# The end of a decoder step on one core: the last attention phase, the samples' row copies and the final layer norms in another order

## The reference

```
def forgetting_attention_mixer(h, k, v, c_k, c_q, q_pos, k_pos, w_in, b_in, w_out, b_out):
    p = h @ w_in + b_in
    q = p[..., :FA_WIDTH].reshape(n, s, FA_HEADS, FA_HEAD_DIM)
    z = p[..., FA_WIDTH:]
    o = ...                      # softmax(q k / 8 + decay) v, block by block
    return (o * jax.nn.silu(z)) @ w_out + b_out
...
x = layer_norm(DEEPNORM_ALPHA * x + (1.0 + gate) * f, ln_g[layer], ln_b[layer])
```

## Time and profile before

| | us |
|---|---|
| median of 3 runs (lowest to highest) | 1718.39 (1717.39 to 1720.2) |
| the profiled execution | 1719.35 |
| its span | 1717.9 |
| PE busy in the span | 1635.8 |
| DVE, ACT, POOL busy | 1008.8, 635.7, 425.1 |

### The profile page before, as it was taken

How to read it: one execution, slowest core, us unless ns; L and a number is a source line. 1 busy time by engine, 2 the same in 40 slices (tenths; PEclk the granted TensorE clock), 3 DMA queues, 4 the chain that set the end, 5 groups by cost and what they waited for, 6 DMA issues and landing times.

```text
span 1717.9 us, 27999 instructions
## 1 busy us (share of the span) xinstructions
PE 1635.8 (95%) x10128; PEld 1425.0 (83%) x10128; DVE 1008.8 (59%) x1564; ACT 635.7 (37%) x1002; POOL 425.1 (25%) x421
## 2 busy tenths in 40 slices
PE   5999999999999998999989999999999999988996
PEld 3899999999999998899977777777778787866764
DVE  3432343334333436424566889788888878688836
ACT  2221221121112115324444545463646363645224
POOL 0250011101101110000221525262626262423130
PEclk9999999999999998999999999999999999999998
DMA  9491112122222220323523242424241422251694
GB/s 371 140 332 49 42 63 87 67 95 76 73 85 74 85 87 24 114 101 108 168 88 118 97 122 88 110 86 112 72 123 61 123 74 86 61 161 44 235 374 170
DMA packets 88674, 199.48 MB, mean 116 GB/s; under 512 B 17106, under 2 KB 47954, under 8 KB 86818
## 3 DMA queue, kind: packets, MB, share of 16 engines
q1 hardware_dynamic: 74898, 139.35, 25.1%
q0 software_dynamic: 13712, 59.30, 9.5%
HBM read 172.88 MB, written 34.39 MB: 121 GB/s over the span
## 4 chain that ended last, share of the span: by engine, by line
PE 77%; DVE 11%; issue 4%; ACT 4%; POOL 2%; DMA 2%; SPq 0%; DVEq 0%; ACTq 0%; POOLq 0%
PE bank L1973 20%; PE bank L1975 19%; PE bank L1974 19%; PE bank L2342 2%; PE bank L2108 2%; PE bank L2344 2%; PE bank L2343 2%; PE bank L2296 2%; DVE bank L1609 2%; PE bank L2324 2%; PE bank L2323 2%; POOL p_lo L726 1%; PE bank L2088 1%; PE bank L2199 1%; DMA xT<-x_t 1%
## 5 line engine op out<-in xcount | busy, mean ns | idle before, releaser
L1973 PE MATMUL bank<-h_hi,w_lo 128*128 128x344 f32 x1152 | 373.8, 324 | 8.6 <-DVE h_lo L1248 8.6
L1974 PE MATMUL bank<-h_lo,w_hi 128*128 128x344 f32 x1152 | 367.9, 319 | 0.0
L1975 PE MATMUL bank<-h_hi,w_hi 128*128 128x344 f32 x1152 | 367.6, 319 | 0.0
L726 POOL TENSOR_TENSOR p_lo<-parg,p_hi 128x512 fp32r<-128x512 f32 (+1 forms) x192 | 229.0, 1210 | 157.5 <-ACT p_hi L1083 157.2
L1973 PEld LDWEIGHTS bank<-h_hi,w_lo 128*128 128x128 f32 x1152 | 216.9, 188 | 13.9 <-issue 9.3
L1973 PE MATMUL bank<-x_hi,w_lo 128*128 128x512 f32 x528 | 219.9, 416 | 0.9 <-DVE x_lo L1683 0.8
L1974 PEld LDWEIGHTS bank<-h_lo,w_hi 128*128 128x128 f32 x1152 | 216.9, 188 | 0.2 <-issue 0.2
L1975 PEld LDWEIGHTS bank<-h_hi,w_hi 128*128 128x128 f32 x1152 | 216.6, 188 | 0.0
L1975 PE MATMUL bank<-x_hi,w_hi 128*128 128x512 f32 x528 | 208.2, 394 | 0.0
L1974 PE MATMUL bank<-x_lo,w_hi 128*128 128x512 f32 x528 | 208.1, 394 | 0.0
L1205 DVE TENSOR_TENSOR w_lo<-raw,w_hi 128x1024 fp32r<-128x1024 f32 x108 | 146.5, 1356 | 80.8 <-ACT w_hi L813 79.7
(11 more groups left out here) (320 smaller groups left out, 2636.5 us busy)
## 6 DMA issues: line engine op xcount, KB each, us to landing
raw<-units SPq DMA_DIRECT2D x124, 512.0 KB, 3.6
scr_k<-cache_k POOLq DMA_DIRECT2D x32, 512.0 KB, 5.7
ada_ring<-w_ada SPq DMA_DIRECT2D x32, 512.0 KB, 3.3
kpb<-scr_k SPq DMA_DIRECT2D x24, 512.0 KB, 4.1
pages<-cache_v POOLq DMA_DIRECT2D x20, 512.0 KB, 6.1
ada_first<-w_ada SPq DMA_DIRECT2D x8, 1024.0 KB, 15.2
ckb<-scr_c POOLq DMA_DIRECT2D x16, 512.0 KB, 4.6
KX<-KA SPq DMA_DIRECT2D x32, 256.0 KB, 6.6
```

The lines of the kernel that those rows point to most:

```text
L726: g.tensor_tensor(p_lo[:, r, off:HALF], parg[:, r, off:HALF], p_hi[:, r, off:HALF].bitcast(F32), ALU.subtract).then_inc(S("p_ready"), 1)
L1973: mm(out, lhs_lo, rhs_hi, start=first, stop=False)
L1974: mm(out, lhs_hi, rhs_lo, start=False, stop=False)
L1975: return mm(out, lhs_hi, rhs_hi, start=False, stop=last)
```

## The change

Four things are written in another order; what is computed is the same.

1. End of the last phase. ACT splits y's part 2 before the last probabilities, and parts 3 to 6 right after them, ahead of the weight unit `hi(U_FA + 1)`; DVE's `lo(U_FA + 1)` goes behind them. Part 7 is split by halves of the tokens: the first before the weight unit (it was divided long before), the second after the last division. `gates(1, ...)` moves ahead of the first half.
2. PE takes part 7 of pieces 0 and 1 apart, with k = 4..6 of piece 2 in between, so that piece 2 has only k = 7 left later.
3. The samples' `tok` copies go from DVE to ACT; the transposes of v and f follow piece 4 and not piece 3.
4. The tail. ACT takes the sums of tiles 3, 4 and 6 (before: 3, 5 and 7), DVE those of 5 and 7. The gate-and-copy of pieces 16 and 17 (`fg2`) comes ahead of the x-hats of tiles 3 and 4, the transposes of tile 7 ahead of the samples' projection, and `sample_rows_act` behind the x-hat of tile 7.

```diff
-        ACT_TILES = (3, 5, 7)
+        ACT_TILES = (3, 4, 6)
         TILE_PAIR = (1, 1, 1, 1, 2, 1, 0, 2)
+        TILE_AFTER = (0, 1, 2, 3, 0, 4, 0, 5)
...
+            def last_y2_high(half):
+                cs = slice(half * HALF, half * HALF + HALF)
+                act.wait_ge(S("o_step"), 8 * KB - 4 + 4 * half)
+                A(y2_hi[:, KB - 3, cs], y2T[:, KB - 1, cs], ACT.Copy).then_inc(S("y2_hi"), 1)
...
                     kq_high(j + 1, 0)
+                else:
+                    y2_high(2)
                 probs(j, 11)
...
                 else:
+                    for k in range(3, KB - 1):
+                        y2_high(k)
+                    last_y2_high(0)
                     hi(U_FA + 1, (U_FA + 1) % 2, (U_FA + 1) // 2 + 1, "mm", 12 * KB)
-                    for k in range(2, KB - 1):
-                        y2_high(k)
                 take_sums(j, 1)
...
-            y2_high(KB - 1)
+            last_y2_high(1)
+            def tok(n, dst, src):
+                act.wait_ge(S("tok_mm"), n)
+                A(dst[:, :], pair(src)[0:NS, :], ACT.Copy).then_inc(S("tok_ready"), 1)
...
+                if m == 2:
+                    tok(1, qtok, 2)
+                    tok(2, ktok, 3)
+                if m == 4:
+                    tok(3, vtok, 2)
...
-                if m in TILE_AT:
-                    if TILE_AT[m] in ACT_TILES:
-                        tile_sums(TILE_AT[m])
+                if m in (11, 12, 13):
                     layer_norm_act(TILE_AT[m], TT, xh2(TILE_AT[m]), "yo_ready")
-            layer_norm_act(6, TT, xh2(6), "yo_ready")
+                if m == 15:
+                    tile_sums(3)
+                if m == 16:
+                    layer_norm_act(3, TT, xh2(3), "yo_ready")
+                    tile_sums(4)
+            for t in (4, 5):
+                layer_norm_act(t, TT, xh2(t), "yo_ready")
+            tile_sums(6)
+            for t in (6, 7):
+                layer_norm_act(t, TT, xh2(t), "yo_ready")
             sample_rows_act()
-            tile_sums(7)
-            layer_norm_act(7, TT, xh2(7), "yo_ready")
...
                 else:
-                    lo(U_FA + 1, (U_FA + 1) % 2)
                     for k in range(2, KB - 1):
                         y2_low(k)
+                    gates(1, "fa_b_out")
+                    last_y2_low(0)
+                    lo(U_FA + 1, (U_FA + 1) % 2)
...
-            gates(1, "fa_b_out")
-            y2_low(KB - 1)
+            last_y2_low(1)
...
                     finish(3)
-                    gated_s()
-                    layer_norm_stats(4, TT)
+                    tile_scale(4)
+            gated_s()
+            layer_norm_stats(5, TT)
             finish(4)
-            tile_scale(5)
-            layer_norm_stats(6, TT)
             finish(5)
+            tile_scale(6)
+            layer_norm_stats(7, TT)
+            finish(6)
             dve.wait_ge(S("fs_used"), 3)
...
-            finish(6)
-            tile_scale(7)
             norm_sum(rS[:, :, :], KB)
             finish(7)
...
-                    fa_first(KB - 1)
+                    pe.wait_ge(S("y2_split"), KB)
+                    fa_step(0, KB - 1).then_inc(S("fa_mm"), 1)
+                    for k in range(KB // 2, KB - 1):
+                        fa_step(2, k)
+                    pe.wait_ge(S("y2_split"), KB + 1)
+                    fa_step(1, KB - 1).then_inc(S("fa_mm"), 1)
...
-                if m == 3:
+                if m == 4:
                     pe.wait_ge(S("tok_ready"), 2)
                     turn(2, 2)
...
             ln_forward(6, r2T, TT)
+            ln_forward(7, r2T, TT)
             pe.wait_ge(S("d_step"), 5)
...
-            ln_forward(7, r2T, TT)
```

More of the change, by code:

```diff
@@ L1545, in y2_low, with last_y2_low @@
                     .then_inc(S("y2_split"), 1)
-            def tok(n, dst, src):
-                dve.wait_ge(S("tok_mm"), n)
-                v.tensor_copy(dst[:, :], pair(src)[0:NS, :]).then_inc(S("tok_ready"), 1)
+            def last_y2_low(half):
+                cs = slice(half * HALF, half * HALF + HALF)
+                dve.wait_ge(S("y2_hi"), KB + half)
+                v.tensor_tensor(y2_lo[:, KB - 1, cs], y2T[:, KB - 1, cs], y2_hi[:, KB - 3, cs].bitcast(F32), ALU.subtract)\
+                    .then_inc(S("y2_split"), 1)
             def by_key(q, c):
@@ L1917, in _ @@
                 if m == 2:
-                    tok(1, qtok, 2)
-                    tok(2, ktok, 3)
                     score_late(4)
                 if m == 3:
-                    tok(3, vtok, 2)
                     score_late(5)
@@ L2131, in ln_forward @@
                 elif n0:
-                    wait(pe, S("ln_hat"), n0 + t if 0 < t < TT // 2 else n0 + t - 1)
+                    wait(pe, S("ln_hat"), n0 + TILE_AFTER[t])
                 else:
@@ L2373, in fa_first @@
                 for half in range(2):
-                    last = fa_step(half, k)
-                    if k == KB - 1:
-                        last.then_inc(S("fa_mm"), 1)
+                    fa_step(half, k)
             def phase(j, more):
@@ L2505, in _ @@
                     pe.wait_ge(S("fg2_ready"), m - 1)
-                    for k in range(KB // 2 if m in (2, 3) else 0, KB):
+                    for k in range({2: KB - 1, 3: KB // 2}.get(m, 0), KB):
                         last = fa_step(m, k)
```

## The result

| | before | changed |
|---|---|---|
| median of 4 runs each (lowest to highest) | 1719.3 (1717.39 to 1721.25) | 1710.32 (1709.78 to 1713.23) |
| the profiled execution | 1719.35 | 1713.23 |
| its span | 1717.9 | 1711.7 |

The measured ratio is 0.9943, with a 95% interval of 0.9929 to 0.9957: faster. The two medians differ by 9.0 us, where 6.1 was forecast; their own quotient is 0.9948. The two profiled executions differ by 6.12 us; the forecast was built on the first of them.

A forecast was written before the change was run, and what follows sets the result against it. PE, busy 1635.8 of 1717.9 us, was taken to bound the kernel, except where unfed or where ACT and DVE set the end. Up to the scores 5.3 plus 0.8 behind gave 6.1 us: 1718.39 to 1712.3, range 1710.0 to 1714.9.

The forecast's parts named there:

- Splits, copies, the head's sum: Up to the scores' transposes: PE waits of 2.2, 0.3 and 2.8 us go, minus 5.3 us, bounds 4.3 and 5.6.
- DVE just follows: DVE's queue up to the gathered scores becomes 5.45 us earlier, enough for PE's 5.3 us to count.
- The division stays at its time: End of the last phase: part 7's first half and the gates fill idle time, moving the last division within 0.1 us.
- Margins: Before the scores: weight unit's low part ready 0.9 us before PE wants it, copy of v 0.8 us before DVE arrives.
- The contention at part 2: y's part 2 on DVE beside POOL's last p_lo costs 0.5 us more, still ahead of PE; sum unchanged.
- Tail: Scores' transposes to the end: minus 2.3 us at full speed, 1.5 given back by a slow samples' fold, minus 0.8.
- Rival A: PE's clock stays up towards the program's end, which gains 2.3 us: 7.6 us in all, 1710.8; chance 0.19.
- B: DVE's extra statistics eat the end's gain and an earlier margin is missed: 3.8 to 5.3 us less, 1713.9; chance 0.24.
- C: Slower: new_key on DVE waits for ACT's copy of v; 8 us late gives 1719.5; chance 0.03.
- D: PE's waits return at the weight unit and scores, the end costs 1 us: some 2 us less, 1716.4; chance 0.04.
- The median of the runs lies 0.96 under the profiled one: Whole kernel: median before taken as 1718.39 us against 1719.35 profiled, so the changed median becomes 1712.3.
- half a microsecond for the median's own spread: Whole kernel: allowance of half a microsecond in the forecast's range, 1710.0 to 1714.9 us.

The follow-up runs named there:

- The copies-only kernel: Kernel before with only the samples' copies moved to ACT and the transposes of v and f behind piece 4; 1716.88 us, ratio 0.9986.
- its repeat: The kernel before run again against itself, no edit; ratio 1.0004, interval 0.9995 to 1.0014.
- the fold on a busy PE: Changed kernel plus 48 unused transposes on PE in the gap ahead of the samples' fold; 1711.48 us, ratio 0.9952 to the kernel before.
- the repeats: The changed kernel run twice more, no edit, against the kernel before; 1714.89 us (ratio 0.9967) and 1713.4 us (ratio 0.9971).

## Why the prediction was wrong, and where it was right

- **Splits, copies, the head's sum: right, 0.3 short.** Forecast 5.3 us, measured 5.64. The step "DVE just follows" came out the other way round: PE waited 0.34 us for `scol` (under 0.3 was forecast), so DVE set S, with 5.64 where its side was put at 5.45, and PE's own gain was near 6.0, more than the 5.3 us of its three waits. One row of each kernel tells why, A to S, the same 245 matmuls at a clock of 1.00; first before, then changed (to the end of the last matmul ahead of S):

```profile
1562.35:1616.13 53.78, 48.41 (x245) 38.89 (x245) 49.30 (x57) 17.80 (x25) 5.61 (x8) 1.00 0.35 126
```

```profile
1562.61:1610.41 47.80, 47.80 (x245) 38.88 (x245) 45.60 (x53) 20.92 (x29) 5.91 (x8) 1.00 0.39 138
```

  Without the three stops PE needs 0.6 us less for the same work: divided by three, an estimate of 0.2 us for each stop beyond the idle time that the list of waits shows. The copies-only kernel, with two of the stops, lies between them: 48.26 us for the same 245. PE's ends are modelled, but the distance from A to S less the listed waits says the same: 48.5 us before, 47.8 after.
- **The division stays at its time: right.** The copy of part 7's second half starts 16.80 us behind A, before it was 16.82.
- **Margins: right.** No wait for `w_lo`, and DVE comes to `new_key` 1.03 us behind the copy of v (0.8 forecast).
- **The contention at part 2: not on DVE.** Part 2 took 1.23 us, not 1.76. Only its last half microsecond lay beside the last `p_lo`, and there POOL's row was the longer one: 1.22 us for two operations, 1.00 in the kernel before and in its repeat. That GpSimd contends with DVE instructions of two SBUF inputs, as the Trainium skill has it (GPSIMD Engine Reference, Key points), changed no sum here; the trace agrees with it at part 1 (1.75 again) and at an operation before it, shown at the end.
- **Tail: right in both terms.** 2.3 us at full clock (2.4 by the fold on a busy PE, with the 0.5 of clock in it that is told there), 1.5 given back by the clock (1.64 in the fold's length; DVE's idle time for the rows, forecast at 1.4 without it, is 3.00), 0.8 forecast and 0.78 measured. Rival A, the clock that stays up, fell in all five profiles of kernels with this tail and its gap unfilled: the fold took 3.58 or 3.59 us. What spoke for it, the wait of 3.2 us that left no mark, was an accident of the one profile; in four of the five other profiles with the old tail, the repeat among them, tile 6's transposes behind that wait ran at the low level. The Trainium skill (TensorE: Matmul & The Clock Gate, Part 1) has the throttled state as the default, which activity lifts; the trace at 1696 (0.50) agrees.
- **Rivals B, C and D: none.** No margin was missed and no transfer took over.
- **The step that failed is the last one of the sum,** "The median of the runs lies 0.96 under the profiled one", with "half a microsecond for the median's own spread". That tie is no property of the kernel. With its fourth run the kernel before had a median 0.05 us under its profiled execution, not 0.96; the changed kernel's median lay 2.9 under, in the repeats 1.5 under and 3.8 over. Single executions of the changed kernel span 1709.65 to 1716.61 over 17 runs (standard deviation 2.4), those of the kernel before 1.7 to 2.1 within a session, so a difference of two medians of four runs carries, by an estimate from these deviations, some 2 us of chance. Of the 9.0 us of the first comparison 6.4 are in the profile, by steps; the other 2.6 are not in the edited code of any of the profiles, and the repeats (5.1 and 5.9 us) do not have them. The range should have had 2 us more on either side. Part of this chance goes with the clock: over three sets of 20 to 24 executions of the kernel before, time and mean granted clock have correlations of -0.69, -0.48 and -0.51, over the 17 of the changed kernel -0.56. The three unprofiled executions of the first comparison had a mean clock of 0.989 to 0.990, the profiled one, the slowest of the four, 0.987, so fewer low spells are the nearest candidate for the 2.6 us. It is not shown: these executions left no trace, and the fastest profile of the changed kernel, 1709.65, has 0.985. Where the 2.6 us arose stays open. The bounds themselves were not quite A and B with half a microsecond either, which would be 1710.3 and 1715.1; 1708.6 lies outside by either.

## What to carry to other kernels

A wait removed from PE is worth what the next meeting point of two engines leaves of it, so price both engines up to there, and price the parts together: here they gave plus 1.1 and minus 3.1 apart, and minus 5.6 together. Where a reordering makes one gap of PE longer, look at what stands behind the gap, since it may run at the lower clock; in this tail filling the gap (1.6 us) or shortening it by moving its releaser ahead (3.1) was worth more than the reordering itself (0.8). Read the clock in more than one profile: here a repeat showed a low spell at a place where the first profile had none. And give a forecast of a median the spread of single executions; in the profiles, a landmark ahead of the edit shows how much of a difference the edit cannot have made.

## What the runs showed of the hardware

- The granted clock fell from 1.00 to about 0.5 (of its levels of 2.4 and 1.2 GHz) during or behind PE's waits of 3.5, 4.7 and 6.7 us, and not behind the one of 2.8 us for the key row. But a wait of 2.4 us near 1020 us was followed by 0.57. The same wait of 3.2 us for the last residual was followed by 1.00 in one execution of the kernel before and by 0.50 in the next, and the same wait of 2.76 us by a fold of 3.38 us in one kernel and of 2.28 in another. The length of the single wait does not settle it.
- Sixteen transposes of 8 rows took 1.91 us at the high level and 3.58 at the low one, the fold 1.95 and 3.59: ratios of 1.87 and 1.84.
- Three two-input operations of DVE stood beside one row of POOL's `p_lo` in the changed kernel. The first, which began 0.09 us ahead of the row, kept its 1.21 us. The other two were slowed: `mb` took 1.23 us, where 0.42 is its time with POOL at rest (the last row below), and the last 1.75, where 1.23 is the lone one's:

```profile
1559.61 5.51 POOL L727 TENSOR_TENSOR p_lo<-parg,p_hi 128x384 fp32r<-128x384 f32 x4 [0.29 <-ACT p_hi L1084]
```

```profile
1559.52 1.21 DVE L1570 TENSOR_TENSOR y_lo<-y2T,y_hi 128x1024 fp32r<-128x1024 f32 x1
...
1561.61 1.23 DVE L1661 TENSOR_TENSOR mb<-mb,maskb 128x256 f32<-128x256 f32 x1
1562.76 1.75 DVE L1570 TENSOR_TENSOR y_lo<-y2T,y_hi 128x1024 fp32r<-128x1024 f32 x1
```

```profile
1526.72 0.42 DVE L1661 TENSOR_TENSOR mb<-mb,maskb 128x256 f32<-128x256 f32 x1
```

  POOL's row was long as well: 5.51 us for four operations, where two of the same size took 1.99 at 1486.69.
